# One-core decoder step: where the square sums of its residual norms are added, and the order of work around them

## The reference, cut to what matters

```python
def rms_norm(x, g):
    xf = x.astype(jnp.float32)
    y = xf * lax.rsqrt(jnp.mean(xf * xf, axis=-1, keepdims=True) + EPS)
    return (y * g.astype(jnp.float32)).astype(x.dtype)
...
        h = rms_norm(x, norm_mix_pre[l])
        ...
        x = x + rms_norm(m, norm_mix_post[l])
        h = rms_norm(x, norm_x_pre[l])
        x = x + rms_norm(cross_attn(l, h, mem_k[l], mem_v[l]), norm_x_post[l])
        h = rms_norm(x, norm_ffn_pre[l])
        f, c = ffn(l, h, ffn_prev[l])
        x = x + rms_norm(f, norm_ffn_post[l])
```

## Time and profile before

| | |
|---|---|
| median of 3 runs (lowest to highest) | 1332.78 us (1331.82 to 1333.16) |
| span of the profiled execution | 1330.2 us |
| TensorE busy | 1230.3 us, 92% |
| VectorE busy | 768.5 us, 58% |
| ScalarE busy | 584.4 us, 44% |
| POOL busy | 294.2 us, 22% |
| mean granted clock of TensorE | 0.971 |
| TensorE idle ahead of the first matmul of a row tile at L392 | 34.8 us |

### The profile page before, as it was taken

How to read it: one execution, slowest core, us unless ns; L and a number is a source line. 1 busy time by engine, 2 the same in 40 slices (tenths; PEclk the granted TensorE clock), 3 DMA queues, 4 the chain that set the end, 5 groups by cost and what they waited for, 6 DMA issues and landing times. The chain is left out here.

```text
span 1330.2 us, 22925 instructions
## 1 busy us (share of the span) xinstructions
PE 1230.3 (92%) x8557; PEld 1091.7 (82%) x8557; DVE 768.5 (58%) x1020; ACT 584.4 (44%) x940; POOL 294.2 (22%) x521
## 2 busy tenths in 40 slices
PE   6999998887999999799999999899998779999995
PEld 4999897587999999699996333599996579999994
DVE  3585735227888733866555665447445167888433
ACT  5456534235655644423345111155434156556442
POOL 4001201114556510200000111003001125564402
PEclk9999999998999999799999999899999789999998
DMA  9647555632545355354444777748647324444440
GB/s 215 234 131 255 188 190 197 251 103 83 171 158 166 126 163 193 105 173 148 142 158 155 272 284 279 255 147 284 226 154 253 138 95 159 158 159 146 150 127 36
DMA packets 177267, 233.64 MB, mean 176 GB/s; under 512 B 5374, under 2 KB 153226, under 8 KB 177200
## 3 DMA queue, kind: packets, MB, share of 16 engines
q1 hardware_dynamic: 159088, 169.09, 39.2%
q0 software_dynamic: 18112, 63.60, 13.6%
HBM read 207.50 MB, written 25.16 MB: 175 GB/s over the span
## 5 line engine op out<-in xcount | busy, mean ns | idle before, releaser
L392 PE MATMUL ps<-hh,wh 128*128 128x288 f32 x1600 | 486.3, 304 | 34.8 <-DVE hl L450 28.2
L327 DVE TENSOR_TENSOR wl<-raw,wh 128x2048 fp32r<-128x2048 f32 (+2 forms) x154 | 331.7, 2154 | 313.4 <-ACT wh L324 313.3
L392 PE MATMUL ps<-hl,wh 128*128 128x288 f32 x1600 | 478.9, 299 | 0.0
L392 PE MATMUL ps<-hh,wl 128*128 128x288 f32 x1600 | 477.0, 298 | 0.0
L324 ACT ACTIVATE wh<-raw 128x2048 fp32r<-128x2048 f32 (+3 forms) x154 | 277.7, 1804 | 296.5 <-PE ps L392 288.0
L392 PEld LDWEIGHTS ps<-hh,wh 128*128 128x128 f32 x1600 | 306.1, 191 | 41.6 <-issue 33.8
L392 PEld LDWEIGHTS ps<-hh,wl 128*128 128x128 f32 x1600 | 308.0, 192 | 0.0
L392 PEld LDWEIGHTS ps<-hl,wh 128*128 128x128 f32 x1600 | 307.5, 192 | 0.3
L392 PE MATMUL ps<-aH,wh 128*128 128x288 f32 x352 | 104.2, 296 | 0.0
L392 PE MATMUL ps<-aL,wh 128*128 128x288 f32 x352 | 103.8, 295 | 0.0
L392 PE MATMUL ps<-aH,wl 128*128 128x288 f32 x352 | 103.6, 294 | 0.0
(11 more groups left out here) (286 smaller groups left out, 1682.3 us busy)
## 6 DMA issues: line engine op xcount, KB each, us to landing
raw<-w_ffn_up SPq DMA_DIRECT2D x44, 1024.0 KB, 5.0
raw<-w_in_odd SPq DMA_DIRECT2D x24, 1024.0 KB, 5.1
ring<-cache_mem_k POOLq DMA_DIRECT2D x16, 1024.0 KB, 5.4
ring<-cache_mem_v POOLq DMA_DIRECT2D x16, 1024.0 KB, 6.2
raw<-state_retention SPq DMA_DIRECT2D x16, 1024.0 KB, 5.2
out<-raw POOLq DMA_DIRECT2D x16, 1024.0 KB, 5.3
raw<-w_ffn_down SPq DMA_DIRECT2D x16, 768.0 KB, 4.4
raw<-w_in_even SPq DMA_DIRECT2D x10, 1024.0 KB, 6.7
```

The lines of the kernel that those rows point to most:

```text
L327: e.tensor_tensor(wl[:, c % 2, 0:kn, :], src, wh[:, c % 2, 0:kn, :].bitcast(F32), ALU.subtract).then_inc(lo_ready, 1)
L392: mm = pe.matmul(out, lhsT, rhs, start=(kc == 0 and n_k == 0 and n == 0), stop=(kc == g.nk - 1 and n_k == kn - 1 and n == 2))
```

## The change

- The pre-norm's sum: `sums_pre` adds the squares of all 8 tiles into the two accumulators by three adds of 128 x 576, and `ssq_pre` needs two groups of matmuls instead of four. At out to xk the three adds stand on POOL, behind `scale_branch`; else on VectorE.
- The post-norm's sum: `sums_post` on VectorE adds tiles 0 to 6 into one accumulator (two adds of 128 x 576, two of 128 x 288), and `ssq_post` needs two groups.
- ScalarE's root table is asked for at the beginning of each branch's last GEMM (`preload_act_table`).
- `add_branch`: VectorE scales tiles 0 and 1, POOL 2 to 7; the low parts follow one tile behind; the split at out to xk stands behind the first low part.
- In a GEMM's first chunk the two column tiles alternate by row tile (`across`), and `ssq_pre` moves from behind the first chunk to between the column tiles of the second (`between`).

```diff
-                     hook=None, need=None):
+                     hook=None, need=None, across=False, between=None):
...
+                    if across and idx == 0:
+                        for j in range(2):
+                            pe.wait_ge(freed, i * 4 + base + j - 3)
+                        for k in range(kn):
+                            need(k)
+                            xh, xl = pairs(k)
+                            for j in range(2):
+                                w_h = wh[:, c % 2, k, j * P:(j + 1) * P]
+                                w_l = wl[:, c % 2, k, j * P:(j + 1) * P]
+                                for n, (lhsT, rhs) in enumerate(((w_h, xh), (w_h, xl), (w_l, xh))):
+                                    mm = pe.matmul(ps[:, j, 0:T], lhsT, rhs, start=k == 0 and n == 0, stop=k == kn - 1 and n == 2)
+                                if k == kn - 1:
+                                    mm.then_inc(w_used, 1)
+                        continue
                     for j in range(2):
                         t = 2 * half + j
                         if kc == 0:
                             pe.wait_ge(freed, i * 4 + base + t - 3)
+                        if between and j == 1:
+                            between(idx)
...
-        def sums(dve, n, part):
+        def sums_pre(e, q):
+            n = 2 * q
+            if n:
+                e.wait_ge(ssq_ready, n)
+            e.wait_ge(sq_ready, CREDIT + 8 * n + 4)
+            e.tensor_tensor(acc[:], sq[:, 0:2, :], sq[:, 2:4, :], ALU.add).then_inc(s("pre_sum"), 1)
+            for part in range(2):
+                e.wait_ge(sq_ready, CREDIT + 8 * n + 6 + 2 * part)
+                e.wait_ge(s("pre_sum"), 3 * q + 1 + part)
+                e.tensor_tensor(acc[:], acc[:], sq[:, 4 + 2 * part:6 + 2 * part, :], ALU.add).then_inc(s("pre_sum"), 1)
+        def sums_post(dve, q, part):
+            n = 2 * q + 1
             if part == 0:
-                if n:
-                    dve.wait_ge(ssq_ready, n)
+                dve.wait_ge(ssq_ready, n)
                 dve.wait_ge(sq_ready, CREDIT + 8 * n + 4)
-                dve.tensor_tensor(acc[:], sq[:, 0:2, :], sq[:, 2:4, :], ALU.add).then_inc(sum_step, 1)
+                dve.tensor_tensor(acc[:], sq[:, 0:2, :], sq[:, 2:4, :], ALU.add).then_inc(s("post_sum"), 1)
+            elif part == 1:
+                dve.wait_ge(sq_ready, CREDIT + 8 * n + 6)
+                dve.wait_ge(s("post_sum"), 4 * q + 1)
+                dve.tensor_tensor(acc[:], acc[:], sq[:, 4:6, :], ALU.add).then_inc(s("post_sum"), 1)
+                dve.wait_ge(s("post_sum"), 4 * q + 2)
+                dve.tensor_tensor(acc[:, 0, :], acc[:, 0, :], acc[:, 1, :], ALU.add).then_inc(s("post_sum"), 1)
             else:
-                dve.wait_ge(sq_ready, CREDIT + 8 * n + 6)
-                dve.wait_ge(sum_step, 2 * n + 1)
-                dve.tensor_tensor(acc[:], acc[:], sq[:, 4:6, :], ALU.add).then_inc(sum_step, 1)
-
-        def ssq(pe, n):
-
-            pe.wait_ge(sum_step, 2 * n + 2)
-            if n:
-                pe.wait_ge(root_ready, n)
+                dve.wait_ge(sq_ready, CREDIT + 8 * n + 7)
+                dve.wait_ge(s("post_sum"), 4 * q + 3)
+                dve.tensor_tensor(acc[:, 0, :], acc[:, 0, :], sq[:, 6, :], ALU.add).then_inc(s("post_sum"), 1)
+        def ssq_pre(pe, q):
+            pe.wait_ge(s("pre_sum"), 3 * q + 3)
+            if q:
+                pe.wait_ge(root_ready, 2 * q)
             pe.matmul(ps[:, BN, 0:T], ones[:], acc[:, 0, :], start=True, stop=False)
-            pe.matmul(ps[:, BN, 0:T], ones[:], acc[:, 1, :], start=False, stop=False)
-            pe.wait_ge(sq_ready, CREDIT + 8 * n + 8)
-            pe.matmul(ps[:, BN, 0:T], ones[:], sq[:, 6, :], start=False, stop=False)
+            pe.matmul(ps[:, BN, 0:T], ones[:], acc[:, 1, :], start=False, stop=True).then_inc(ssq_ready, 1)
+        def ssq_post(pe, q):
+            pe.wait_ge(s("post_sum"), 4 * q + 4)
+            pe.wait_ge(root_ready, 2 * q + 1)
+            pe.matmul(ps[:, BN, 0:T], ones[:], acc[:, 0, :], start=True, stop=False)
+            pe.wait_ge(sq_ready, CREDIT + 8 * (2 * q + 1) + 8)
             pe.matmul(ps[:, BN, 0:T], ones[:], sq[:, 7, :], start=False, stop=True).then_inc(ssq_ready, 1)
...
-            for t in range(1, DT):
+            for t in range(2, DT):
...
-            dve.wait_ge(m_ready, DT * q + 1)
-            dve.tensor_tensor(mT[:, 0, :], mT[:, 0, :], rstd[:], ALU.mult).then_inc(s("scaled_first"), 1)
-            for t in range(DT + 2):
-                if t < DT:
-                    if t == 0:
-                        dve.wait_ge(s("scaled_first"), q + 1)
-                    else:
-                        dve.wait_ge(scaled, (DT - 1) * q + t)
-                    dve.scalar_tensor_tensor(out=xT[:, t, :], in0=mT[:, t, :], scalar=gain(t),
-                                             in1=xT[:, t, :], op0=ALU.mult,
-                                             op1=ALU.add).then_inc(x_ready, 1)
-                if t >= 2 and q < 3 * DEPTH - 1:
-                    dve.wait_ge(x_ready, DT * (q + 1) + t - 1)
-                    gained_low(dve, q + 1, t - 2)
-                if t == 3 and not late:
-                    splits()
+            def add(t):
+                if t < 2:
+                    dve.wait_ge(m_ready, DT * q + t + 1)
+                    dve.tensor_tensor(mT[:, t, :], mT[:, t, :], rstd[:], ALU.mult).then_inc(s("scaled_first"), 1)
+                    dve.wait_ge(s("scaled_first"), 2 * q + t + 1)
+                else:
+                    dve.wait_ge(scaled, (DT - 2) * q + t - 1)
+                dve.scalar_tensor_tensor(out=xT[:, t, :], in0=mT[:, t, :], scalar=gain(t),
+                                         in1=xT[:, t, :], op0=ALU.mult,
+                                         op1=ALU.add).then_inc(x_ready, 1)
+            def low(t):
+                if q < 3 * DEPTH - 1:
+                    dve.wait_ge(x_ready, DT * (q + 1) + t + 1)
+                    gained_low(dve, q + 1, t)
+            add(0)
+            add(1)
+            low(0)
+            if not late:
+                splits()
+            for t in range(2, DT):
+                add(t)
+                low(t - 1)
+            low(DT - 1)
             if late:
                 splits()
-            if q < 3 * DEPTH - 1:
-                sums(dve, 2 * q + 2, 0)
-                sums(dve, 2 * q + 2, 1)
+            if late and q < 3 * DEPTH - 1:
+                sums_pre(dve, q + 1)
...
-                     hook=lambda i, idx: ssq(pe, 2 * q) if idx == 0 else None)
+                     across=True, between=lambda idx: ssq_pre(pe, q))
...
+            act.preload_act_table(ACT.Sqrt)
             run(act, g, True, evac, 0, 1)
...
-                    sums(dve, 2 * q + 1, half)
+                    sums_post(dve, q, half)
...
             run(dve, g, False, evac, 1, 2, hold=True)
+            sums_post(dve, q, 2)
...
-            ssq(pe, 2 * q + 1)
+            ssq_post(pe, q)
...
                 scale_branch(pool, 3 * l)
+                sums_pre(pool, 3 * l + 1)
...
-                    sums(dve, 2 * q, 0)
-                    sums(dve, 2 * q, 1)
+                    sums_pre(dve, 0)
...
-                ssq(pe, 2 * q + 2)
+                ssq_pre(pe, q + 1)
```

More of the change, by code:

```diff
@@ L1788, in _ @@
                          need=lambda k: pe.wait_ge(s("mem_lo"), 8 * l + k + 1),
-                         hook=lambda i, idx: ssq(pe, 2 * q + 1) if idx == 0 else None)
+                         hook=lambda i, idx: ssq_post(pe, q) if idx == 0 else None)
                 products(pe, G["k", l], mem, s("k_nat"), CREDIT + 8 * l, natural=True, i0=1, i1=2)
-                ssq(pe, 2 * q + 2)
+                ssq_pre(pe, q + 1)
                 pe.wait_ge(s("k_nat"), CREDIT + 8 * l + 8)
@@ L1840, in _ @@
                 pe.sem_inc(s("a_free"), 1)
-                ssq(pe, 2 * q + 5)
+                ssq_post(pe, q + 2)
             for n in range(6):
```

## The result

| | before | after |
|---|---|---|
| median | 1332.97 us (4 runs, 1331.82 to 1334.16) | 1348.19 us (4 runs, 1346.40 to 1351.17) |
| span of the profiled execution | 1330.2 us | 1349.5 us |
| mean granted clock of TensorE | 0.971 | 0.957 |

The change made the kernel slower by 15.2 us: the ratio is 1.0116, with a 95% interval of 1.0099 to 1.0133. The forecast was 8.7 us more, 1341, with a range up to 1348; the third rival, in which the clock stays low for longer, said 1349. The sign and the mechanism were right; the sizes of two terms, the clock and the sum of the waits, were not. The profiled execution of after is the longest of the four, so its 19.3 us over the first trace of before are more than the medians' 15.2.

What follows compares the result with a forecast made beforehand. TensorE was taken as busy for 92% of the span, so only places where it stands still could change. Waits +1.9 and clock +6.8 made +8.7 on 1332.78, or 1341 us; range 1330 to 1348.

Steps and rivals of the forecast that it cites:

- the third rival: At the five new rests and in_odd, two stretches at half clock each are lost: +16 us, 1349; chance 0.15.
- the clock: Behind four of five new rests (start, both v, both up) a 3.4 us stretch at 0.50 costs 1.7 us: +6.8.
- the sum of the waits: Over the whole kernel, gains and new waits without the clock's answer come to +1.9 us.
- Start: At the program's start the root comes 1.9 us later, at 33.1, and TensorE rests about 2.5: +1.35 us.
- Memory's root: In layer 0's memory part the root's table load leaves TensorE's path: -1.3 us, once.
- Down: In each down GEMM the earlier table load exceeds 0.9 us of slack at the second chunk: +0.4 us per layer.
- Up: Ahead of each up GEMM, 4 us won early mostly become a 2.9 us wait before chunk 3: -0.75 us each.
- In_odd: Ahead of in_odd chunk 3 moves with the root, and its wait grows to about 5 us: -0.55 us.
- Out to xk: From out to xk, two of POOL's three wide adds hold VectorE's chain 1.05 us each: +2.1 us per layer.
- End: At the program's end two ones-matmul groups go (-1.0); with earlier accumulation -1.1 us.
- The first: All rests leave the clock at 1.00, so only the waits' +1.9 counts: 1334.7 us; chance 0.17.
- The second: At out to xk POOL's adds cost nothing (4.2 us gone) and the clock holds: -2.3, 1330.5 us; chance 0.13.

Runs made afterwards that it cites:

- the filled kernel: The changed kernel with unread matmuls filling all five new rests and in_odd's, including 36 and 16 at each out to xk: 1335.11 us.
- after, second trace: The changed kernel run once more for a second trace, with no edit: 1345.99 us.
- the first filled kernel: The changed kernel with unread matmuls in the new rests and in_odd's, only 28 at each out to xk, leaving 0.73 and 1.95 us of rest there: 1342.20 us.
- second trace of before: The kernel before run once more for a second trace, with no edit: 1333.81 us.
- the best version: Changed kernel with sums, ones-matmuls and table load moved, v's first split put ahead, v's first chunk waiting only for its two banks: 1311.57 us.

## Why the prediction was wrong

Two terms of the sum were too small: the clock, +6.8, and the waits, +1.9. What the runs showed, place by place, by the starts of the weight copies against the first trace of before (us; the forecast's waits stand first; the filled kernel shows the waits with the clock held at the new rests):

| place | waits, forecast | all rests filled | after | after, second trace |
|---|---|---|---|---|
| start | +1.35 | +2.3 | +3.4 | +1.1 |
| root of the memory's norm | -1.3 | -1.3 | -1.3 | -1.3 |
| out to xk, layer 0 and 1 | +2.1, +2.1 | +2.5, +2.4 | +4.3, +4.7 | +4.5, +4.5 |
| attention, layer 0 and 1 | none | -1.2, -2.7 | +1.5, +0.9 | +0.9, +0.8 |
| xo to up, layer 0 and 1 | -0.75, -0.75 | -0.3, -0.2 | +2.4, +1.4 | +1.5, +1.4 |
| down's second chunk, layer 0 and 1 | +0.4, +0.4 | +0.8, +0.8 | +0.8, +0.8 | +0.8, +0.8 |
| down to in_odd | -0.55 | -1.0 | +0.7 | -0.5 |
| end of the program | -1.1 | -0.1 | -0.4 | -0.4 |
| span | +1.9 | +2.1 | +19.3 | +14.1 |

**The clock: the first step that failed.** "I take four of five, at 1.7 each": 6.8, or 13.6 us at half clock. In the first trace of after all five new rests were followed by 0.50, three of them for 6.8 to 10 us and not 3.4, and in_odd's stretch grew from 3.4 to 6.7: 34 us at half clock, and the filled kernel is 11 us shorter at these places. In the second trace four of five were followed by 0.50, as forecast, but both v for 6.8 us, and in_odd's stretch was the longer one again: 24 us, and at out to xk, up and in_odd the filled kernel is 8 us shorter than this trace. The price of one stretch was about right: up in layer 1, with one of 3.4 us behind its third chunk, is 1.5 us longer in after than in the first filled kernel. It was the length and number of the stretches that I had too low. I had one row of a stretch behind a short rest (562.30) and took its length for all; the row at up, 1086.80 to 1090.20 at 0.50 with TensorE already back at work, may have been the better model for places where a second wait follows soon, as at v (4.02 and then 1.44 us); no run tests that. And the 2.40 us that I took as held at full clock fell in the second trace of before: one trace had shown one of two answers.

**The sum of waits: the second step that failed.** +1.9 was forecast. The filled kernel's +2.1 agrees by luck: without the attention it is +6.0, and 5 to 6 is what the waits cost (the start alone differs by 0.4 us between the two traces of before), or up to 7.7 with in_odd's old stretch taken out. Nearly every term was too low, by up to 1 us. And the attention, for which the sum had no term, took 2.4 us more in the first trace of after and 1.7 in the second; no run shows why. Term by term:

- Start: rest 2.5 forecast, 2.45 measured, and root 33.1 forecast, 33.66 measured. The place cost +1.1 in the second trace of after, where the clock held, and +2.3 in the filled kernel, against +1.35.
- Memory's root: -1.3, measured -1.28; right.
- Down: +0.4 forecast, +0.80 measured in both layers; the slack was half of what I read. No drain was seen: ScalarE's copy follows the load at once (475.69 + 1.28, then 476.98). The Trainium skill, page "ScalarE: Activation LUTs", section on what ACT_TABLE_LOAD costs, adds a drain to each switch; it was rightly left out of the sum.

```profile
475.69 1.28 ACT L580 ACT_TABLE_LOAD   x1
...
476.98 1.28 ACT L324 ACTIVATE wh<-raw 128x1280 fp32r<-128x1280 f32 x1
```

- Up: chunk 2 at R+13.85, root +18.2, chunk 3 +24.15, rest 2.9 were forecast; +13.6, +18.1, +24.1, 2.90 measured; right. R itself came 0.53 us sooner, not 0.7, and the filled kernel won 0.3 and 0.2 at the place, not 0.75.
- In_odd: the rest of about 5 was 5.05, but the root came no sooner in the first trace (forecast 0.55; 0.4 in the second). The post-norm's root had won nothing there: TensorE's sum waited 2.12 us for VectorE's additions, against 1.06 before, which is what the two groups fewer had won. The place was +0.7 with its second stretch at 0.50.
- Out to xk: +2.1 forecast from adds that hold VectorE 1.05 each; 1.16 measured, and +2.45 and +2.49 us at v's first split in the two layers. The place in the chain was right. What I called k's third chunk is its last. I also held that TensorE's groups behind POOL's sums cost nothing; they waited 4.02 us, within the time that v's weights took anyway, but as a rest for the clock. The Trainium skill, page "SBUF — State Buffer", section on the two sides of SBUF, has whichever of VectorE and GpSimd starts first lock the other out for its whole instruction. The trace agrees: VectorE's operations end 0.31 and 0.32 us behind POOL's (152.57 and 152.26; 155.44 and 155.12). The two holds come to 2.3 us, between my 2.1 and the 2.8 that I gave for a whole lock (its terms, 1.05 and 0.44, make 1.49 an add and 3.0 in all).
- End: the groups gave 0.97 as forecast (from the first group to the root 1.25 us, in the earlier trace rows 2.22), but VectorE's scaling of tile 1 stands ahead of the second transposed tile, which I had not put on the path. That tile comes 7.18 us behind the first group, before 7.19: nothing is left of the 0.97, and the -0.4 measured (-1.1 forecast) comes from behind it. After, and the second tile before:

```profile
1327.84 0.72 PE L464 MATMUL ps<-acc,ones 128*128 128x288 f32 x2 [0.30 <-PE ps L409]
...
1329.09 0.50 ACT L470 ACTIVATE root<-ps,small 128x288 f32<-128x288 f32 x1 [0.80 <-PE ps L466]
...
1335.02 0.47 PE L607 MATMUL ps<-ident,xT 128*128 128x128 f32 x1 [1.45 <-DVE xT L513]
```

```profile
1315.36 0.48 PE L556 MATMUL ps<-ident,xT 128*128 128x128 f32 x1 [0.49 <-DVE xT L472]
```

**The rivals.** The first (clock holds, 1334.7) is close to the filled kernel's 1335.1 by the same luck as the sum of waits. The second (POOL's adds are free) is out: they held VectorE for 2.3 us. The third (1349) came by its time, with a chance of 0.15; of its mechanism, two stretches at every place, the first trace shows three places of five and the second two, and larger waits made up for the others. The range ended 0.2 us below the median.

## What to carry to other kernels

A rest that is moved is not a rest that is gone: where a sum stands behind more matmuls, ask when its root lets the next weights through, before counting what the earlier chunk wins. On a kernel whose TensorE is busy nearly all the time, price a new rest at what it delays plus one stretch or more at half clock behind it, and fill the rest with idle matmuls once to see which of the two is the larger. Then compare the two kernels place by place and not by their totals: here the attention, in which nothing was changed, moved by up to 4 us a layer, enough to make a wrong sum look right. The largest step of the best version came not from shorter work but from taking what TensorE waits for (a weight split, a copy out of a bank) out from behind a chain that TensorE doesn't need.

## What the runs showed of the hardware

- The same rest brought the clock down in one execution and not in another of the same program: 2.40 and 2.38 us at k's last chunk in the kernel before, with 1.00 and 0.50 behind it; 2.45 us at the start of after, with 0.50 and 1.00.
- In the kernel with the wide adds on VectorE up's third chunk rests 2.90 us as in after, and the 6 us behind it are at 1.00, where after has 0.50; in layer 1 of the same trace it rests 2.87 us, and 6.8 us are at 0.50:

```profile
335.00:341.00 6.00, 6.00 (x46) 6.00 (x46) 6.00 (x11) 3.85 (x8) 3.33 (x6) 1.00 0.61 181
...
1115.60:1122.20 6.60, 5.74 (x24) 5.74 (x25) 6.60 (x12) 4.76 (x8) 4.14 (x6) 0.50 0.46 159
```

- POOL's 576-wide addition took 1.53 to 1.56 us, and VectorE's 0.51 us operation beside it 1.66 to 1.68. The third addition at each place, with VectorE's chain over, took 1.47 and 1.48.
